# Compression attention and block choice moved from a stage of their own into the attention list

## The reference, cut to what matters

```python
def compress(a, pos, w1, b1, w2):                       # MLP: 2048 -> 256 -> 64 for each of 127 pieces
    blocks = blocks + pos[None, None, :, None, :]
    flat = blocks.transpose(0, 1, 3, 2, 4).reshape(n, nc, G, CMP_LEN * hd)
    return jax.nn.gelu(flat @ w1 + b1) @ w2

def nsa_mixer(...):
    kc = compress(kc_raw, pos, k_w1, k_b1, k_w2)
    vc = compress(vc_raw, pos, v_w1, v_b1, v_w2)
    s = jnp.where(c_valid, s - slopes[:, :, None, None] * c_dist, -jnp.inf)      # s = q . kc * scale
    p_cmp = p / jnp.where(den > 0, den, 1.0)
    o_cmp = jnp.einsum('ngrtc,ncgd->ntgrd', p_cmp, vc.astype(jnp.float32))
    imp = jnp.einsum('ngrtc,cs->ngts', p_cmp, jnp.asarray(block_overlap(nc, ns)))
    score = jnp.where(valid, jnp.where(forced, jnp.inf, imp), -jnp.inf)
    _, idx = lax.top_k(score, n_sel)
    ...                                                  # o_slc: attention over the chosen blocks
    o_win, _ = banded_attention(q, kw, vw, WIN_A - 1, slopes, 1)
    o = g[..., 0:1] * o_cmp + g[..., 1:2] * o_slc + g[..., 2:3] * o_win.astype(jnp.float32)
```

## Time and profile before

| | |
|---|---|
| median of 3 runs | 3938.0 us (3937.69 to 3938.13) |
| profiled execution | 3936.96 us, of which the span from first to last instruction is 3935.2 us |
| busy in the span | PE 3538.7 us (90%), PEld 2818.5, DVE 1432.5, ACT 1167.8, POOL 435.5 |
| mean granted clock of TensorE | 0.933 of full speed |

### The profile page before, as it was taken

The page is one execution under the profiler, slowest core; times in us unless marked ns, Lnnn a source line. Parts: engine busy times, 40 slices in busy tenths (PEclk is TensorE's granted clock), DMA queues, the critical chain, the costliest instruction groups (busy, mean ns, idle before and its releaser), DMA issues. The chain is left out here.

```text
span 3935.2 us, 45798 instructions
## 1 busy us (share of the span) xinstructions
PE 3538.7 (90%) x16642; PEld 2818.5 (72%) x16642; DVE 1432.5 (36%) x3939; ACT 1167.8 (30%) x2055; POOL 435.5 (11%) x317
## 2 busy tenths in 40 slices
PE   5999999939538899999999796999999999999997
PEld 4888888836536787565566585888788878887886
DVE  4111101111325456666665343441154034304421
ACT  4111111101225556444454232331133023203310
POOL 2545444400000000000000100000000000000000
PEclk7999999967558989999999898999999999999999
DMA  5877766580249996224210466656655665656553
GB/s 177 283 269 264 268 210 202 200 211 11 55 96 192 197 208 136 62 61 105 59 33 6 156 211 224 219 195 229 229 195 194 226 232 194 232 187 232 195 188 124
DMA packets 328278, 685.37 MB, mean 174 GB/s; under 512 B 117344, under 2 KB 182496, under 8 KB 312544
## 3 DMA queue, kind: packets, MB, share of 16 engines
q1 hardware_dynamic: 296896, 536.04, 45.3%
q0 software_dynamic: 31168, 146.48, 10.3%
HBM read 502.41 MB, written 180.03 MB: 173 GB/s over the span
## 5 line engine op out<-in xcount | busy, mean ns | idle before, releaser
L1740 PE MATMUL f_banks<-f_h_hi,f_w_hi 128*128 128x512 f32 x1408 | 549.2, 390 | 33.0 <-DMA f_w_lo<-f_lo 25.3
L1740 PE MATMUL f_banks<-f_h_lo,f_w_hi 128*128 128x512 f32 x1408 | 548.5, 390 | 0.0
L1740 PE MATMUL f_banks<-f_h_hi,f_w_lo 128*128 128x512 f32 x1408 | 548.5, 390 | 0.0
L322 PE MATMUL z_banks<-z_h_hi,z_w_hi 128*128 128x512 f32 x1056 | 416.2, 394 | 4.6 <-POOL z_w_lo L203 4.6
L322 PE MATMUL z_banks<-z_h_lo,z_w_hi 128*128 128x512 f32 x1056 | 412.4, 390 | 0.0
L322 PE MATMUL z_banks<-z_h_hi,z_w_lo 128*128 128x512 f32 x1056 | 411.8, 390 | 0.0
L1164 PE MATMUL a_ot_ps<-a_turned_w,a_vs 128*65 128x256 f32 (+3 forms) x1452 | 404.7, 431 | 0.6 <-issue 0.6
L1132 PE MATMUL a_s_ps<-a_k_hi,a_q 128*128 128x256 f32 (+3 forms) x696 | 271.4, 396 | 113.2 <-DVE a_peak L1280 40.7
L1164 PEld LDWEIGHTS a_ot_ps<-a_turned_w,a_vs 128*65 128x65 f32 x1452 | 200.1, 144 | 189.1 <-issue 153.0
L1740 PEld LDWEIGHTS f_banks<-f_h_hi,f_w_hi 128*128 128x128 f32 x1408 | 264.8, 188 | 90.8 <-issue 31.5
L1740 PEld LDWEIGHTS f_banks<-f_h_lo,f_w_hi 128*128 128x128 f32 x1408 | 264.7, 188 | 55.1
(11 more groups left out here) (183 smaller groups left out, 5170.8 us busy)
## 6 DMA issues: line engine op xcount, KB each, us to landing
f_w_hi<-f_hi SPq DMA_DIRECT2D x264, 512.0 KB, 3.6
f_w_lo<-f_lo SPq DMA_DIRECT2D x264, 512.0 KB, 4.5
z_xs<-in_w_ffn POOLq DMA_DIRECT2D x33, 1024.0 KB, 8.8
f_hi<-z_v_hi POOLq DMA_DIRECT2D x33, 1024.0 KB, 5.1
f_lo<-z_xs POOLq DMA_DIRECT2D x33, 1024.0 KB, 6.4
z_hi<-z_st_hi SPq DMA_DIRECT2D x92, 256.0 KB, 3.7
z_lo<-z_st_lo SPq DMA_DIRECT2D x92, 256.0 KB, 5.0
a_k_hi<-z_hi SPq DMA_DIRECT2D x36, 512.0 KB, 10.7
```

The lines of the kernel that those rows point to most:

```text
L322: last = pe.matmul(banks[:, 4 * k + n, :], w[:, k, c, :], h[:, c, tok], start=(c == 0 and q == 0), stop=(c == DC - 1 and q == 2))
L1740: last = pe.matmul(banks[:, bank, :], w[:, s % RING, c * P:(c + 1) * P], h[:, c, :], start=(c == 0 and x == 0), stop=(c == DC - 1 and x == 2))
```

## The change

- `project` stores blocks 31 and 32 once, as plain float32 (`z_raw`), instead of as high and low part.
- `compressed` becomes `compress`: loads, MLP, and nothing else. Its keys and values (`kc_hi`, `kc_lo`, `vk` with the block overlap beside it) stay in SBUF for `attend`.
- The compression's attention becomes six units of kind "k", one a head, with one key block each, that stand ahead of every two dilated heads: k, b, b, k, b, b, and so on. A "k" unit loads a query and a bias table, no keys and no values, and stores its result like a "c" unit.
- The block choice is cut in four parts a group (`choose`, `turn_choice`), at steps 5 and 7 of each four tiles in the unit after the last "k" head of the group; POOL stores the result.
- The first load of the chosen blocks (`load_qm`) moves from the start of `attend` to SP's turn of the first "w" unit.

```diff
         def is_value(j):
             return V0 <= j < V0 + NV
+        def is_plain(j):
+            return j >= V0 + NV
...
+                    if is_plain(j):
+                        sp.wait_ge(zhi_done, 4 * j + n + 1)
+                        sp.dma_start(z_raw[j - V0 - NV, :, n * 512:(n + 1) * 512], st_hi[:, n, :].bitcast(F32))\
+                            .then_inc(stored[n], 16)
+                        continue
...
-def compressed(nc, ident, z_hi, z_lo, v_nat, pos_t, w1, b1_t, w2, overlap, cmp_bias, pick_bias, o_nat, sel_t):
+def compress(nc, z_raw, pos_t, w1, b1_t, w2, overlap, kc_hi, kc_lo, vk):
...
+            sp.dma_start(poss[:], pos_t).then_inc(small_in, 16)
+            sp.dma_start(b1s[:], b1_t).then_inc(small_in, 16)
+            for m in range(2):
+                sp.dma_start(w1s[:, m], w1[m].rearrange("(c p) n -> p c n", p=P)).then_inc(w1_in[m], 16)
+                for g in range(G):
+                    for odd in range(2):
+                        sp.dma_start(x2[odd * HD:(odd + 1) * HD, m, g, 0:T - odd],
+                                     z_raw[m, g * HD:(g + 1) * HD, odd:T]).then_inc(x2_in[m], 16)
+            for dup in range(2):
+                sp.dma_start(kw2[:, :, dup, :], w2[0].rearrange("(m p) n -> p m n", p=P)).then_inc(small_in, 16)
+            sp.dma_start(vw2[:], w2[1].rearrange("(m p) n -> p m n", p=P)).then_inc(small_in, 16)
...
+            pe.wait_ge(small_in, 16 * 5)
...
+    units = []
+    for h in range(6):
+        units.append(Unit("k", h, 1, 0, h * HD, None, None))
+        units += pairs[2 * h:2 * h + 2]
...
+    for g in range(G):
+        last = heads.index(("k", g * R + R - 1))
+        for q in range(4):
+            chosen_at[(last + 1) * NT + 4 * q + 7] = (g, q)
...
             for u in range(NU):
+                if u == first_chosen:
+                    load_qm(u + 1)
...
+            def turn_choice(g, q):
+                b = pick_batch[g, q]
+                old = batches[b - TB]
+                pe.wait_ge(unsel_done, 4 * g + q + 1)
+                pe.wait_ge(taken[old["eng"]], old["count"])
+                for i in range(4):
+                    last = pe.transpose(t_ps[0:NS, b % TB, i, :], unsel[:, 4 * q + i, :], idt[:])
+                last.then_inc(turned, 1)
...
+                elif unit.kind == "k":
+                    dve.tensor_scalar(coef[:].unsqueeze(2), on[:, :, HD:HD + 1], 1e-30, None, ALU.max).then_inc(chain, 1)
+                    dve.wait_ge(chain, at + 1)
+                    dve.reciprocal(coef[:], coef[:]).then_inc(chain, 1)
+                    dve.wait_ge(chain, at + 2)
+                    dve.tensor_tensor(gcoef[:].unsqueeze(2), coef[:].unsqueeze(2), gate[:, i:i + 4, 3 * unit.h:3 * unit.h + 1],
+                                      ALU.mult).then_inc(chain, 1)
+                    share = on_ps[:, :, HD + 1:HD + 1 + NS]
+                    part = imp[:, i:i + 4, :] if unit.h % R == 0 else shares[:]
+                    dve.tensor_tensor(part, share, coef[:].unsqueeze(2).to_broadcast([P, 4, NS]), ALU.mult).then_inc(chain, 1)
+                    dve.wait_ge(chain, at + 4)
+                    if unit.h % R:
+                        dve.tensor_tensor(imp[:, i:i + 4, :], imp[:, i:i + 4, :], shares[:], ALU.add).then_inc(chain, 1)
+                        dve.wait_ge(chain, at + 5)
+                    dve.tensor_tensor(rows[:, :, 0:HD], on[:, :, 0:HD], gcoef[:].unsqueeze(2).to_broadcast([P, 4, HD]),
+                                      ALU.mult).then_inc(out_done, 1)
...
+            def choose(g, q):
+                tiles, count = slice(4 * q, 4 * q + 4), 4 * g + q
...
+                for i in range(4 * q, 4 * q + 4):
+                    dve.max(top[:, i, :], score[:, i, :]).then_inc(top_done, 1)
...
+                for i in range(4 * q, 4 * q + 4):
+                    dve.match_replace(picked[:, i, :], top[:, i, :], score[:, i, :], PICKED).then_inc(picked_done, 1)
...
             for n in range(N + 4):
+                if n + 2 in chosen_at:
+                    choose(*chosen_at[n + 2])
```

More of the change, by code:

```diff
@@ L267, in _ @@
                     normalise(t + 2)
-            for j in range(NZ):
+            for j in range(V0 + NV):
                 for n in range(4):
@@ L466, in _ @@
             sp.dma_start(vw2[:], w2[1].rearrange("(m p) n -> p m n", p=P)).then_inc(small_in, 16)
[L467 to L471, removed]
+            sp.wait_ge(zeroed, 3)
             for g in range(G):
[L473 to L492, removed]
@@ L688, in scores @@
-            def scores(g, i):
-                slot = i % 2
-                if i >= 2:
-                    pe.wait_ge(biased, NT * R * g + NT * R + R * (i - 1))
-                for r in range(R):
-                    for part, k in enumerate((k_hi, k_lo)):
-                        last = pe.matmul(s_ps[:, slot, r * P:(r + 1) * P], q2[:, r, i * P:(i + 1) * P], k[:, g, :],
-                                         start=(part == 0), stop=(part == 1))
-                last.then_inc(qk_done, 1)
@@ L719, in turn_sel @@
[L719 to L740 removed]
+        @blk.scalar
@@ new lines, in _ @@
+        def _(act):
+            for m in range(2):
+                act.wait_ge(hb_done, m + 1)
+                for half in range(2):
+                    act.wait_ge(hid_done, 2 * m + half + 1)
+                    act.activation(h1[:, m, half, :], hid[:, 2 * m + half, 0:G * NC], ACT.Gelu_apprx_tanh,
+                                   bias=hb[:, m, half:half + 1]).then_inc(gelu_done, 1)
+            act.wait_ge(zeroed, 3)
+            act.wait_ge(kc_done, 1)
+            act.activation(kc_hi[:, :, 0:NC], kc_ps[:, 0:G * NC].rearrange("p (g c) -> p g c", g=G),
+                           ACT.Copy).then_inc(khi_done, 1)
@@ L752, in __init__ @@
         for t in range(NT):
-            if self.chosen:
+            if kind == "k":
+                self.tiles.append([0])
+            elif self.chosen:
                 self.tiles.append(list(range(t + 1)))
@@ L774, in attention_units @@
 def attention_units():
-    units = []
+    pairs = []
     for pair, fold in enumerate(FOLDS):
@@ L871, in attend @@
     weigh_at = [[n for n in range(N) if min(issue[n] + 1, n) == s] for s in range(N)]
-    steps = {"b": 1, "c": 2, "w": 3, "s": 3}
-    links = [sum(steps[kind[x // 4]] for x in range(g)) for g in range(N // 4)]
+    pick_batch = {batch["pick"]: b for b, batch in enumerate(batches) if "pick" in batch}
+    steps = {"b": 1, "c": 2, "w": 3, "s": 3, "k": 5}
+    links = [sum(steps[kind[x // 4]] - (kind[x // 4] == "k" and units[x // 4].h % R == 0) for x in range(g))
+             for g in range(N // 4 + 1)]
     own_step = kind.index("w") * NT + 4
+    first_chosen = kind.index("w")
     mix_steps = [(kind.index("w") + x) * NT + y for x in range(1, 9) for y in (4, 12)]
@@ L913, in attend @@
         o_b = sb("o_b", [P, 2, 4, HD])
+        spare = turned_w[:, 0, 2 * NT:, :].rearrange("p (a b) q -> p a (b q)", b=4)
+        imp, pick, score, picked, unsel = (spare[:, x].rearrange("p (t s) -> p t s", s=NS) for x in range(5))
+        top = spare[:, 5, 0:8 * NT].rearrange("p (t s) -> p t s", s=8)
         s_ps = ps("s_ps", [P, SB, 512])
@@ L1163, in weigh_values @@
                     at = (has[0] % 4) * P
-                    last = pe.matmul(ot_ps[0:HD + 1, at:at + count * P], vs[:, s, kb, :], rows,
+                    values = vk[:, unit.h // R, :] if unit.kind == "k" else vs[:, s, kb, :]
+                    last = pe.matmul(ot_ps[0:out_width(g), at:at + count * P], values, rows,
                                      start=(x == 0), stop=(x == len(blocks) - 1), skip_group_check=True)
@@ L1264, in bias @@
                     dve.wait_ge(own_done, 1)
+                    for out in sel_out:
+                        dve.wait_ge(out, 64)
                     dve.wait_ge(far_in, 16 * far_at.of_unit[u] + 16)
@@ L1274, in bias @@
                 at = (unit.back + 1) * P - whole
-                floor = nsink[:, unit.h:unit.h + 1] if unit.kind == "c" else 3e38
+                if unit.kind == "k":
+                    table, at = near[:, near_at.slot[near_at.of_unit[u]], 0:CW], 8 * (NT - 1 - t)
+                floor = nsink[:, unit.h:unit.h + 1] if unit.kind == "c" else 1e20 if unit.kind == "k" else 3e38
                 for j, (a, z) in enumerate(cuts):
```

425 lines of the change are left out of this document (134 added, 291 removed).

## The result

The changed kernel takes 3819.4 us (median of 4 runs, 3818.3 to 3826.1) against 3937.9: ratio 0.9705, 95% interval 0.9688 to 0.9722. The forecast was 3827, in a range of 3786 to 3860. The profiled execution lasted 3826.1 us, its span 3824.3, 110.9 us less than the span before.

What follows compares the result with a forecast made beforehand. Taken as bounds: loads, then a chain of short steps in stage two; PE and DMAs almost equally in the dilated heads. 3936.96 - 20.5 - 183.0 - 1 + 94 = 3826.5 us, given as 3827, range 3786 to 3860.

Steps and rivals of the forecast that it cites:

- the three stretches ahead of the mixed section: Up to the third stage's first load: -1 for `project`, -20.5 for MLP loads, -183.0 for attention and choice leaving.
- the mixed section: Third stage, first bias to first bias with `nsink`, dilated and "k" heads together: 239.6 us growing by 94 to 334.
- Loads of the MLP: Second stage, first load to PE's first MLP product: fewer bytes at 228 GB/s, 37.8 us against 58.3, -20.5.
- The third stage's start: From the stage's first load to its first bias: same bytes ahead of `sink`, so 41.9 us kept, change 0.
- The "k" heads: Mixed section: 24 groups at 4.7 us undisturbed, 4.86 with the clock, 117 us in all, bounds 113 and 132.
- The supplement for the clock: In "k" groups: neighbours' clock of about 0.9 raises 4.7 us to 4.86, a fifth of the way to 5.5.
- the 29 us of waits in the dilated heads are hidden by the 'k' heads between them: Mixed section: computation of 334 us exceeds transfers of 286, so late-data waits in the dilated heads vanish.
- Choice: Block choice on DVE within dilated heads: half of its 13 us counted, +7, bounds 0 and 13.
- First load of the chosen blocks: Moved behind SP's late turns: lands 4 to 5 us before the product needing it, so 0.
- Transfers as the bound: Rival: "k" heads hide beneath transfers in the mixed section, 286 us, time 3779; chance 0.13.
- The "k" heads in full: Rival: "k" heads add fully, dilated heads keep their pace; section 360 to 391 us, time 3853 to 3884; chance 0.22.
- The lower clock throughout: Rival: TensorE falls to its lower clock in the whole mixed section, 510 us, time 4003; chance 0.03.

Runs made afterwards that it cites:

- the early weights: Changed kernel with the MLP's second-layer weight loads moved ahead of the compress stage's large loads: 3804.2 us, ratio 0.9661.
- the longer finish: Changed kernel with two more DVE steps, into a tile nothing reads, in each k group's finish: 3833.4 us, ratio 0.9726.
- three table slots: Changed kernel with three slots instead of two for the bias tables of kinds k, b and c: 3805.7 us, ratio 0.9667.
- the three edits: Changed kernel with three bias-table slots, sinks and gates loaded early, and second-layer MLP weights loaded early: 3765.2 and 3765.6 us.
- the order of three and six: Changed kernel with three k heads then six dilated heads, twice, instead of one k head before every two dilated: 3847.7 us, ratio 0.9774.

## Why the prediction was right

*The bound and the sum.* Every stretch moved in the forecast direction. That the profiled execution, 3826.1 us, meets the sum of 3826.5 is luck, for the errors cancel: the three stretches ahead of the mixed section gave 6.6 us more than forecast (-211.1 against -204.5), the section took 7.5 us more. The excess ahead of it is the shorter end of `project` (3.8 us against 1), the boundary behind the MLP (933.59 less some 932.8 where DVE's last copy ends, against 3.7 us), and loads at a little over the rate used.

*Loads of the MLP.* Right in kind and size, 36.3 us against 37.8. The experiment with the early weights shows what they really were: a wait for the last of all loads, of which 23 us were never needed.

*The third stage's start.* "The same bytes stand ahead of `sink`" held to 0.2 us. I kept it as given; 29 us of it were only a place in a queue.

*The "k" heads.* The undisturbed group was forecast at 4.7 us and measured 4.64; the longer finish confirms that DVE's finish counts in full there. The term as a whole was too small: 341.1 us less the 204 of the dilated heads leave 137 us, where 117 stood in the sum with 132 as the upper bound. The mean distance was 5.9 us, and 5.1 with three table slots. The supplement for the clock, up to 4.86, came from the neighbours' 0.9 and left out the waits: in the same 24 us the clock was 0.79 with the wait for a table and 1.00 without. Yet the late tables are not the whole of it. With three slots, where DVE waits for no table, it still fell in later "k" heads, as far as 0.84 in the fifth; no run shows why.

```profile
1196.00:1218.00 22.00, 17.19 (x77) 11.64 (x76) 11.29 (x61) 8.88 (x22) 0.00 (x0) 0.84 1.07 202
```

*The step that failed in part* is that "the 29 us of waits in the dilated heads are hidden by the 'k' heads between them". They left the dilated heads, which fell to 204 us, where 210 + 7 were forecast. But "k" heads took up to 8.5 us more than four undisturbed groups, in part from a cause that I hadn't looked for: not the mean bandwidth, of which 16% was free, but a table of 0.13 MB behind 2.1 MB of keys in one queue. Removing that shortened the section by 16 us. That the section was off by only 7.5 us is luck again: some 20 too little for the "k" heads, 13 too much for the dilated heads with the choice.

*Choice.* +7 forecast, half of 13 to 14 us. The search alone, some 10 us of it, cost 3.9: a little under the half that was taken.

*First load of the chosen blocks.* Right: issued at 1436.1 us, the first product with it at 1445.34 shows no wait for a load.

*The rivals.* Transfers as the bound with a section of 286 us did not occur. With the three edits, which start the section earlier, it holds 65.6 MB instead of 58.6 at a share of 0.98, so the transfers nearly fill it again; PE is busy for 87% there too, and which of them sets its length is not shown. The "k" heads in full, 360 us or more, is the number that the order of three and six gave (362.1), but not for that rival's reason: in the mixed order one dilated head still follows another six times, and PE's view there has none of the waits put down to "issue". The lower clock throughout did not come: 0.86 in the section.

## What to carry to other kernels

A short chain taken out of a stage of its own is worth its whole length there, and costs in its new place what it adds to the loop that sets the pace: count its steps in that loop one by one. When transfers stop being the bound on average, look at the order in which each one lands: a small load behind large ones makes the engine wait although the queues have room, and a third buffer that lets it be issued a turn earlier takes that away. Loads that release the first instruction of a stage belong ahead of those that merely come early in the program; three such edits gave another 59 us here, until the transfers nearly filled the section again.

## What the hardware showed that I had not expected

One wait of 3.9 us for a table cost a "k" head 1.7 times its length: its last two groups took 6.7 us more than two undisturbed ones (8.51 + 7.48 against 2 x 4.64), and the granted clock of the 24 us fell to 0.79; without the wait they took 0.8 us more than undisturbed ones. That is a local price: over this head and the two behind it the kernel with three slots gained only 0.4 us, since another wait took the place of the first. And a table of 131 KB took 14.1 us to land behind 2.1 MB of keys, when the DMAs were full just there, whatever the section's mean:

```profile
1026.00:1044.00 18.00, 11.44 (x72) 7.92 (x71) 7.66 (x44) 6.86 (x18) 0.00 (x0) 1.00 1.08 213
```
